# Gated-delta decays from transferred rows of summed gates, ahead of the forgetting attention, and five shifted steps

## The reference

```
# block 1
h = rms_norm(x); proj = h @ w_in            # q, k, v, three conv streams, two gates
y_att = stick_breaking_attention(q, k, v) @ w_att_branch     # 8 heads of 64
x = x + rms_norm((sig(g_att)*y_att + sig(g_conv)*y_conv) @ w_out)
x = x + rms_norm((gelu(g) * a) @ w_down)    # a, g = conv(rms_norm(x) @ w_up)

# block 2
u = rmsnorm(x); proj = u @ w_in             # gdn q,k,v,z, alpha, beta, fox q,k,v,f, two gates
g = -exp(a_log) * softplus(ga + dt_bias)    # log gate of 8 gdn heads
# gated delta rule: G = cumsum(g)
decay = where(t >= s, exp(G[t] - G[s]), 0)  # per head
A = beta * (k k^T) * decay; solve (I + A);  o = (q k^T * decay) v_new + ...
# forgetting attention: softmax(q k^T * scale + cum[t] - cum[s]) v, 8 heads of 128
h = x + merged @ w_out
x = h + square(relu(rmsnorm(h) @ w_up)) @ w_down
```

## Time and profile before

| | us |
|---|---|
| median of 3 runs | 919.85 (917.68 to 924.02) |
| the profiled execution | 917.21 |
| its span, first to last instruction | 915.5 |
| PE busy | 893.9 |
| DVE busy | 572.9 |
| ACT busy | 498.8 |
| POOL busy | 137.9 |

### The profile page before, as it was taken

The page is one execution under the profiler, slowest core; times in us unless marked ns, Lnnn a source line. Parts: engine busy times, 40 slices in busy tenths (PEclk is TensorE's granted clock), DMA queues, the critical chain, the costliest instruction groups (busy, mean ns, idle before and its releaser), DMA issues.

```text
span 915.5 us, 15641 instructions
## 1 busy us (share of the span) xinstructions
PE 893.9 (98%) x6455; PEld 830.5 (91%) x6455; DVE 572.9 (63%) x823; ACT 498.8 (54%) x771; POOL 137.9 (15%) x151
## 2 busy tenths in 40 slices
PE   8999999999999999999999899999999999999998
PEld 8898999889999988788898788999999899998886
DVE  4556554778887845665577786865376665554442
ACT  5576864556556634566656664333454565554330
POOL 6011101611111100133353110000010002210000
PEclk9999999999999999999999999999999999999999
DMA  8743364665655557355544344632346556666560
GB/s 284 262 152 112 98 228 155 217 201 193 205 189 163 194 195 265 103 197 176 160 131 150 112 137 141 188 105 92 93 142 203 185 162 192 200 205 188 185 205 23
DMA packets 132442, 155.27 MB, mean 170 GB/s; under 512 B 9337, under 2 KB 106004, under 8 KB 132244
## 3 DMA queue, kind: packets, MB, share of 16 engines
q1 hardware_dynamic: 125844, 151.78, 50.9%
q10 hardware_dynamic: 6528, 2.50, 1.1%
HBM read 152.03 MB, written 2.24 MB: 169 GB/s over the span
## 4 chain that ended last, share of the span: by engine, by line
PE 83%; DVE 8%; ACT 4%; DMA 3%; issue 1%; POOL 1%; SPq 0%; ACTq 0%; POOLq 0%
PE ps L1952 71%; PE ps L1915 3%; PE ps L1983 3%; PE ps L2208 2%; PE ps L1912 2%; DVE wl L824 2%; DVE gkq L858 2%; ACT wh L1410 1%; DMA raw<-in_w_in 1%; DMA U<-blocks 1%; DMA blocks<-last 1%; DVE mt L1256 1%; DMA Yc<-inverses 1%; ACT gkq L1614 1%; DVE sS L1058 0%
## 5 line engine op out<-in xcount | busy, mean ns | idle before, releaser
L824 DVE TENSOR_TENSOR wl<-raw,wh 128x1024 fp32r<-128x1024 f32 (+1 forms) x275 | 326.4, 1205 | 183.6 <-ACT wh L1410 183.3
L1952 PE MATMUL ps<-xh,wh 128*128 128x256 f32 x1280 | 362.9, 284 | 0.7 <-ACT xh L1458 0.7
L1952 PE MATMUL ps<-xh,wl 128*128 128x256 f32 x1280 | 354.7, 277 | 0.6 <-POOL wl L666 0.6
L1952 PE MATMUL ps<-xl,wh 128*128 128x256 f32 x1280 | 351.4, 277 | 0.0
L1410 ACT ACTIVATE wh<-raw 128x1024 fp32r<-128x1024 f32 (+1 forms) x292 | 286.8, 1025 | 112.2 <-PE ps L1952 90.1
L1952 PEld LDWEIGHTS ps<-xh,wh 128*128 128x128 f32 x1280 | 241.2, 188 | 3.4 <-issue 1.4
L1952 PEld LDWEIGHTS ps<-xh,wl 128*128 128x128 f32 x1280 | 240.5, 188 | 0.9 <-POOL wl L666 0.8
L1952 PEld LDWEIGHTS ps<-xl,wh 128*128 128x128 f32 x1280 | 239.4, 188 | 0.4
L666 POOL TENSOR_TENSOR wl<-raw,wh 128x1024 fp32r<-128x1024 f32 (+1 forms) x17 | 44.5, 2619 | 85.9 <-ACT wh L1410 85.3
L1952 PE MATMUL ps<-wh,f2L 128*128 128x512 f32 x128 | 49.8, 389 | 0.0
L1952 PE MATMUL ps<-wh,f2H 128*128 128x512 f32 x128 | 49.8, 389 | 0.0
(11 more groups left out here) (323 smaller groups left out, 1385.6 us busy)
## 6 DMA issues: line engine op xcount, KB each, us to landing
raw<-in_w_in SPq DMA_DIRECT2D x55, 1024.0 KB, 5.0
raw<-in_w_up SPq DMA_DIRECT2D x38, 1024.0 KB, 5.2
raw<-in_w_down SPq DMA_DIRECT2D x26, 1024.0 KB, 5.0
raw<-in_w_out SPq DMA_DIRECT2D x8, 1024.0 KB, 5.0
raw<-in_w_proj_fox SPq DMA_DIRECT2D x4, 1024.0 KB, 5.0
raw<-in_w_proj_gdn SPq DMA_DIRECT2D x4, 1024.0 KB, 5.0
raw<-in_w_conv_branch SPq DMA_DIRECT2D x4, 512.0 KB, 3.4
raw<-in_w_att_branch SPq DMA_DIRECT2D x4, 512.0 KB, 3.4
```

Source lines behind the costliest of these rows:

```text
L824: e.tensor_tensor(L, R, H.bitcast(F32), ALU.subtract).then_inc(lo.sem)
L1952: k = e.matmul(o, l, r, start=opens, stop=done and n == ends[c], skip_group_check=True)
```

## The change

1. `small`: PE also sums g for 8 heads into PS[4][0:8, 256:512] (two matmuls with `UI`). `CX` becomes (8, 2, 256); DVE copies the new rows beside the negated ones; `sums` has two parts. ACT writes both with one DMA, and then issues two spreading DMAs, first the new `GR` (128 x 8 x 256, the sums of g), then `CS`. `GR` lies in memory that `obH` takes later.
2. `decays`: PE's part is gone (16 matmuls), and with it the waits on PS[7]. DVE and ACT read `GR` where they read PS[7]. The rounds stand at `decays_at(r)` = 4 + 10 r, counted from the start of `U_FQ + 6`, two units before `U_FV`.
3. `attention` (block 1): on DVE, `sp_` stands one tick earlier.
4. Before `norm(1)`: the low half of `U_UP + 1` moves from between the two `scaled` steps to tick 5 of `U_WO + 3`.
5. `gdn`: PE's products of head h (h < 3) wait for squares round 5 + h, not for the last round 7.
6. `level_at` and `solve_at` are 2 ticks later.
7. `o_turn` begins at tick 3 of `U_G2 + 1`, not 2.

```diff
 def decays_at(r):
-    return 23 + 22 * r
+    return 4 + 10 * r
 def level_at(c, i):
-    return 71 + 2 * c + 8 * i
+    return 73 + 2 * c + 8 * i
 def solve_at(g):
-    return 102 + 2 * g
+    return 104 + 2 * g
...
-        CX = reg("CX", [NH, T], 57.25)
+        CX = reg("CX", [NH, 2, T], 56.25)
+        GR = reg("GR", [P, NH, T], 60, place=MOVES)
-        sums = nc.dram_tensor("sums", [NH, T], F32)
+        sums = nc.dram_tensor("sums", [2, NH, T], F32)
...
             for n in range(2, 8, 2):
+                if n == 6:
+                    side.add(decays())
...
-                    yield from pause(6)
+                    yield from pause(5)
                     e.wait_ge(*att_act[s]("ln", i))
...
-                    yield from pause(5)
+                    yield from pause(6)
                     e.wait_ge(*att_pe[s]("c", i))
...
-                e.tensor_scalar(CX[:], PS[4][0:NH, 0:256], -1.0, None, ALU.mult).then_inc(sdv.sem)
+                copy(CX[:, 1, :], PS[4][0:NH, 256:512]).then_inc(sdv.sem)
+                e.tensor_scalar(CX[:, 0, :], PS[4][0:NH, 0:256], -1.0, None, ALU.mult).then_inc(sdv.sem)
...
-                    yield from at.to(decays_at(r) + 1)
+                    yield from at.to(decays_at(r))
-                    e.wait_ge(*epe("e", r))
+                    e.wait_ge(gates_in, 16)
...
+            def first_post(i):
+                if i:
+                    low(U_UP + 1, 1)
+                post(0, U_WO + 2 * i + 1, i, 0)
...
-            low(U_UP + 1, 1)
...
-                unit(U_G2 + i, 2 if i == 1 else None, lambda: side.add(o_turn()))
+                unit(U_G2 + i, 3 if i == 1 else None, lambda: side.add(o_turn()))
...
-                e.dma_start(CS[:].rearrange("p h t -> p (h t)"), sums[:].rearrange("h t -> (h t)").partition_broadcast(P)
-                            ).then_inc(sums_in, 16)
+                for dst, k, landed in ((GR, 1, gates_in), (CS, 0, sums_in)):
+                    e.dma_start(dst[:].rearrange("p h t -> p (h t)"), sums[k].rearrange("h t -> (h t)").partition_broadcast(P)
+                                ).then_inc(landed, 16)
...
-                    for j in range(4):
-                        k = e.matmul(PS[7][:, j * P:(j + 1) * P], G_g[:, a, 4 * h4 + j:4 * h4 + j + 1].broadcast_to([P, P]),
-                                     UI[:], start=True, stop=True)
-                    k.then_inc(epe.sem)
...
-                        e.wait_ge(*gns("s", 7))
+                        e.wait_ge(*gns("s", 5 + h))
```

More of the change, by code:

```diff
@@ L360, in two_blocks @@
         fox_dve = [steps(f"fox_dve{i}", "b0", "b1", "mask", "r0", "r1", "rec", "ol") for i in range(2)]
-        sums_out, sums_in = (sem(n) for n in ("sums_out", "sums_in"))
+        sums_out, sums_in, gates_in = (sem(n) for n in ("sums_out", "sums_in", "gates_in"))
         gca = steps("gdn_conv_act", "y0", "y1")
@@ L797, in gpsimd @@
                 side.add(fox_norm(n + 1))
-            side.add(decays())
             for u in range(U_FV, U_GK + 8):
@@ L1263, in vector @@
                 unit(u - 1)
-                unit(u, 5, lambda u=u, i=i: post(0, u, i, 0))
+                unit(u, 5, lambda i=i: first_post(i))
                 post(0, u, i, 1)
             scaled(1, 0)
-            low(U_UP + 1, 1)
             scaled(1, 1)
@@ L1564, in decays @@
                                 k = e.activation(E0[:, h, P + 64 * n:P + 64 * n + 64],
-                                                 PS[7][:, j * P + 64 * n:j * P + 64 * n + 64], ACT.Exp,
+                                                 GR[:, h, P + 64 * n:P + 64 * n + 64], ACT.Exp,
                                                  bias=G_cross[:, n, h:h + 1])
@@ L2093, in small @@
                 e.wait_ge(*sdv("lf"))
-                e.wait_ge(*cst("uf"))
+                e.wait_ge(*cst("ui"))
                 mul(ps4[0:NH, 0:128], G_lf[:, 0, :], UF[:], True, True)
                 mul(ps4[0:NH, 128:256], G_lf[:, 0, :], ones[:], True, False)
-                mul(ps4[0:NH, 128:256], G_lf[:, 1, :], UF[:], False, True).then_inc(spe.sem)
+                mul(ps4[0:NH, 128:256], G_lf[:, 1, :], UF[:], False, True)
+                for a in range(2):
+                    k = mul(ps4[0:NH, 256 + a * P:256 + (a + 1) * P], G_g[:, a, :], UI[:])
+                k.then_inc(spe.sem)
                 yield
@@ L2106, in small @@
                 mul(ps5[:, 40:48], ONE0[:], G_g[:, 1, :], False, True).then_inc(spe.sem)
-            def decays():
-                at = Ticks()
-                for r in range(4):
-                    yield from at.to(decays_at(r))
-                    a, h4 = r // 2, r % 2
-                    if r:
-                        e.wait_ge(*edv("d", r - 1))
-                    else:
-                        e.wait_ge(*fnk("fin", 7))
-                    if r > 2:
-                        e.wait_ge(*ecr("c", r - 3))
-                    for j in range(4):
-                        k = e.matmul(PS[7][:, j * P:(j + 1) * P], G_g[:, a, 4 * h4 + j:4 * h4 + j + 1].broadcast_to([P, P]),
-                                     UI[:], start=True, stop=True)
-                    k.then_inc(epe.sem)
             def fox_norm(n):
@@ L2335, in tensor @@
             for u in range(U_GZ, U_YG):
-                unit(u, XH, XL, at=2 if u == U_G2 + 1 else None, begins=lambda: side.add(o_turn()))
+                unit(u, XH, XL, at=3 if u == U_G2 + 1 else None, begins=lambda: side.add(o_turn()))
             for i in range(4):
```

7 lines of the change are left out of this document (3 added, 4 removed).

## The result

| | us |
|---|---|
| changed kernel, median of 9 executions | 911.25 (909.94 to 915.65) |
| kernel before, median of 9 beside it | 923.31 (917.68 to 924.80) |
| ratio | 0.9904, 95% interval 0.9881 to 0.9927 |
| profiled execution of the changed kernel | 909.94, span 908.2 |

The kernel got faster, within the range of 902.5 to 914, but by a little less than the 1% that a measurement tells. In the two profiled executions, against which the sum was made, it gains 7.3 us of span where the sum had 11.1: 909.94 us, where 906.1 was forecast for such an execution.

The account below looks back on a forecast made before the run. PE, busy 893.9 of 915.5 us, was taken as the bound. Gains 7.2 + 1.6 + 1.2 + 0.6 + 0.5 = 11.1 us took the profiled 917.21 to 906.1; adding 1.8 gave 907.9 us, 8-in-10 range 902.5 to 914.

Parts of the forecast that it names:

- The decays: Part 1, fp32 rounds off PE and exps off ACT's path to `sT`: gain 7.2 us, bounds 5.0 and 11.1.
- To this I add 0.4 for DVE and POOL ahead of the third pair: Low half and the rounds' DVE work and masks before the third head pair: gain 0.4 us, between 0 and 0.8.
- So I follow ACT: ACT's chain to `sT`: 2.1 us earlier at the third head pair, another 3.8 at the fourth, together 5.9.
- so the 1.36 us come back too: Fourth head pair: with about 1 us of PE idle time left, the clock no longer falls, gaining 1.36 us.
- Where the rounds go: Decay rounds' new places on ACT and DVE: what they push back costs nothing; 2.1 us if cover were gone.
- The fourth pair: Fourth head pair: `sT` another 3.8 us earlier, about 1 us of PE idle time left there.
- The five steps: Parts 2 to 5: heads' products 1.6, `level_at` 1.2, `sp_` 0.6, low half before `norm(1)` 0.5 us, `o_turn` and `solve` nothing.
- level steps: `level_at` 2 ticks later moves twelve matmuls ahead of PE's wait for `Yt`: gain 1.2 us, from 0 to 1.2.
- The transfer: `GR` lands at 412.0 or 416.9, before DVE wants it at 422: no cost, a microsecond for each later than 422.
- The rival that made it slower: `GR` shares DMA engines with `CS` and the weight stream and DVE waits: landing at 450 gives 928 us; chance 0.04.
- the attention's chain sets the pace, and the clock still falls: Rival: decays give 5.0 us, level step nothing, sum 7.5, so 911.5 us; chance 0.22.
- The third rival: `sT` stays late by the work on the units; PE gets 3.1 from the rounds, 1.5 elsewhere: 915.3 us; chance 0.04.

Follow-up runs that it names:

- e10: Changed kernel with four rounds of four fp32 matmuls that nobody reads put back on PE at the decay rounds' old ticks: 907.26 us, ratio to before 0.9843.
- e15: Changed kernel with only the second of the four removed rounds put back on PE as four useless matmuls (tick 45 of `U_FV`): 909.77 us, ratio to before 0.9887.
- e6: Changed kernel with DVE's multiply-adds of the third gdn k unit two ticks later, so its low half stands ahead of them: 911.91 us, ratio to before 0.9922.
- e4: Changed kernel with DVE's reciprocals four ticks earlier, ahead of a unit's multiply-adds and low half: 907.57 us, ratio to before 0.9875.
- e13: Changed kernel run again, unaltered, in a later group beside two kernels with useless PE matmuls put back: 910.86 us, ratio to before 0.9911.
- e8: Changed kernel with decay rounds 2 and 3 at ticks 29 and 47 in place of 24 and 34: 912.20 us, ratio to before 0.9924.
- e5: Changed kernel run once more, unaltered, beside three variants on one chip: 913.07 us, ratio to before 0.9940.
- e2: Kernel before with edits 3 to 7 (the five shifted steps), decays untouched, PE's part of `o_turn` at tick 2: 914.38 us, ratio to before 0.9962.
- e9: Changed kernel with `level_at` and `solve_at` back at 71 and 102, `o_turn` left at 3: 913.62 us, ratio to before 0.9921.
- e7: Changed kernel with eight fp32 matmuls that nothing reads on PE ahead of the third head pair's transposes: 909.60 us, ratio to before 0.9912.
- e1: Changed kernel with edits 3 to 7 taken back, the decays alone (PE's part of `o_turn` stayed at tick 3): 918.92 us, ratio to before 1.0011.
- e3: Changed kernel with POOL's four masks alone back at their old ticks: 912.27 us, ratio to before 0.9939.

## Why the prediction was right and wrong

**The decays, 7.2 us; measured 3.2 by the ledger**, below even my lower bound of 5.0. This is the term that was wrong, and the place is the third head pair. From behind `norm(1)` to the third pair's products I had a gain of 2.1 + 0.4 - 0.45 = 2.05 us; the ledger shows a loss of 2.10 (-1.66 to +0.44). From there to the fourth pair I had 3.8 and it shows 4.08; for the fall of the clock behind it 1.36 and 1.21. At the third pair two steps failed, the first two of this list.

- *"To this I add 0.4 for DVE and POOL ahead of the third pair."* I took the 2.00 us low half of the earlier trace rows for one that would come down to 1.22 once the masks were gone. But it was waiting for a low half of POOL's, not for a mask. It went up to 3.35, since POOL, no longer held up there, had reached its next half. The sum had +0.4, the runs show a loss of 1.35 for this half alone (3.35 less 2.00), and e10 and e15 show that it is decided by which of two engines starts first; DVE started 0.10 us behind POOL. The Trainium skill, "SBUF — State Buffer", section "Who interferes with whom", says that a VectorE instruction with two SBUF inputs contends with a GpSimd instruction that reads SBUF, and that issue order, not op shape, decides who blocks. I quoted the first of these for norm(1) and applied neither here. The traces agree: DVE's half ends 1.09 us behind POOL's in the changed kernel and in e6, and takes 1.21 to 1.22 where it starts first (e4, e10, e15), while POOL's then takes 3.0 in place of 2.4.
- *"So I follow ACT. At the third pair sT comes 2.1 us earlier."* The principle, that a faster PE would meet the attention's pace, was right: the removed rounds turned into the wait at the transposes that I named. But I followed ACT only from the normalization on. Its start hangs on DVE's reciprocal, and ACT had stood idle for it already before:

```profile
490.56 1.50 ACT L1600 ACTIVATE sS<-sS,stt 128x128 f32<-128x128 f32 x4 [2.32 <-DVE stt L1067]
```

  This row stands just ahead of the earlier trace rows, and I did not follow it back. DVE's chain (low half, scores, unit work, reciprocal) sets the pace of the third pair, and nothing in the change shortens it. The scores began 1.22 us later (480.99, 482.21), and so did the normalization and PE's transposes (1.20 and 1.21). PE's products with `sT` came 0.44 us later instead of 2.1 earlier, though PE had 1.9 in hand before the wait (1.00 at the second pair's transposes, 471.69 and 470.69, and 0.89 for the round behind them). e4 shows the reciprocal's part: with it earlier, the wait is gone.
- The clock, *"so the 1.36 us come back too"*. The fourth pair's fall is gone, worth 1.2 in the ledger; a fall at the third cost 1.4. The 1.4 is read from the distance between the third pair's transposes and its products: 5.28 us in the changed kernel, 3.83 in e13's profiled execution, which has the same wait and no fall. By itself the clock gave about -0.2 in place of +1.36.
- *"Where the rounds go ... I cost them at nothing."* The two added matmuls cost 0.38 (0.45 forecast). The rounds' new places cost 1.06 in front of the scores of the first pair; at its transposes the ledger loses 0.9 (-1.00 to -0.11, behind them), the 0.9 that I had forecast there. DVE's work of round 2 took 2.42 us and not 1.38, as it met POOL's mask of round 1 (in e8, with no mask beside it, it took 1.38); ACT waited 0.96 us for it, and its exps stood ahead of the copy of `fqm`:

```profile
433.29 2.42 DVE L1026 TENSOR_SCALAR gp<-GR,gv__83 128x64 f32<-128x64 f32 x8
```

```profile
432.78 1.73 POOL L719 TENSOR_TENSOR fg<-fg,uf 128x512 f32<-128x512 f32 x1
```

```profile
434.11 0.67 ACT L1590 ACTIVATE fqm<-ps,cols 128x512 f32<-128x512 f32 x1
435.74 2.02 ACT L1572 ACTIVATE fg<-GR,gv__83 128x64 f32<-128x64 f32 x8 [0.96 <-DVE gp L1026]
...
438.66 0.67 ACT L1590 ACTIVATE fqm<-ps,cols 128x512 f32<-128x512 f32 x1
```

  I had named the bound (2.1 us if the cover is gone) and not used it. e8 took the two waits away, which shows that they were the rounds'. But the end of e8 is e5's: the third pair and `Yt` took what was gained, so this cost is not what made the kernel miss.
- *The fourth pair* came out as forecast: `sT` waits 0.64 us there, and the wait shrank by 3.9 (3.8 in the text).

**SBUF or PSUM as source.** For eight exps of 64 columns the estimate from the rule of the Trainium skill that the prediction quotes ("VectorE: DVE Perf Modes", section "The TRN2 errata — SBUF-src ops pay a fixed extra latency per instruction") was 0.35 us more from SBUF. The 2.02 us against the 1.75 of the earlier trace rows are 0.27 more, so the trace agrees in sign and roughly in size. DVE's eight took 1.38 undisturbed against 1.62: less, as the rule says, but by a third of its 0.78.

**The five steps, 3.9 us; measured 4.0.** By the ledger: `sp_` 0.95 (0.6), low half 0.64 (0.5; POOL's pow at 187.70 took 0.55 us in place of the 1.41 of the earlier trace rows), heads 1.23 (1.6; 1.98 came at the first head, and 0.75 went again within three heads, where PE waits 0.45 for DVE's `last`), level steps 1.2 (1.2), `o_turn` and `solve` nothing. e2 confirms the sum, 3.5 us. The level steps' share is the least sure: e9 took them back, and its profiled execution has no wait for `Yt`; its time, 0.5 to 2.8 us higher, does not settle their size.

**The transfer.** `GR` landed 6.5 us after its issue at 407.23, so at 413.7, and DVE's first round began at 419.80 without idle time. The rival that made it slower had no part.

**The rivals.** The one that happened is "the attention's chain sets the pace, and the clock still falls", 7.5 us and 911.5. It is right in kind and, partly by luck, in its sum: its decays gave 5.0 (measured 3.2) and its level step nothing (1.2), and the fall came at another pair. I gave it 0.22 where it deserved the most. The sign was in my own text, that the third pair's transposes wait already, and I took it for a small effect. The third rival has an error of adding: its own terms, 3.1 and 1.5, make 4.6 us and 914.4, not 915.3.

**The own tests.** Two of the conditions under which I called the prediction wrong came true: the clock fell, and PE's waits from 440 to 520 come to just over 4 us (3.4 and 0.64).

## What to carry to other kernels

Before a removed wait or a removed matmul is counted, follow the late operand back over every engine, not only over the one that produced it last: here it was DVE, two steps behind ACT. Where two engines share a port, look up which one starts first and by how much; here 0.1 us behind POOL cost DVE 2.1 us, and four matmuls on a third engine flipped the order. And when a kernel with less work is not faster, put the work back as a filler: it is a cheap test of whether it was on the path, though it also moves the other engines, as e15 shows.

## What was not expected of the hardware

**Two paces of PE at one granted clock.** The span of one kernel differs by 4 to 5 us between executions in which nothing else differs. In e6's profiled execution (914.55 us) PE fell behind steadily from 190 to 310, in the units of `U_UP`. The windows of the changed kernel's profiled execution, and of e6's:

```profile
240.00:260.00 20.00, 20.00 (x179) 20.00 (x178) 16.12 (x24) 12.61 (x19) 2.63 (x2) 1.00 0.57 186
```

```profile
240.00:260.00 20.00, 20.00 (x172) 20.00 (x172) 15.33 (x23) 11.28 (x19) 3.08 (x2) 1.00 0.54 177
```

179 matmuls in 20 us against 172, without a gap and at a granted clock of 1.00: starts 0.113 or 0.118 us apart, 4%, over the whole stage and worth 4.5 us there. Other stages do the same in other executions (the units at 740 to 820 in e2). What sets the pace of a stage was not tried. It makes a median of few executions uncertain by some 0.5%: the median of before moved from 918.2 to 923.3 between groups while its lowest time stayed within 0.4 us.

**The clock's fall is not told by the length of one wait.** PE idled 4.6 us at the fourth pair of before and the clock fell, 2.0 at the third and it didn't; from that I judged by the length of a wait. But it fell behind 1.76 us in e6 and behind 1.99 in e2, and in e13's profiled execution it stayed at 1.00 behind 3.10:

```profile
490.00:495.00 5.00, 2.08 (x16) 1.84 (x17) 2.68 (x8) 3.08 (x8) 2.59 (x1) 1.00 0.22 63
495.00:500.00 5.00, 5.00 (x43) 4.89 (x42) 3.46 (x7) 3.75 (x9) 2.94 (x1) 1.00 0.43 150
```

Each fall lasted 3.4 us (6.8 once, in e4). Those of 3.4 us cost 1.1 to 1.6 us: from the third pair's transposes to its products it is 3.8 us without a fall (e7, e13, e15), 4.9 to 5.4 with one (e1, e3, e5, e6, e8, e9).
